# Cross attention of prompt and samples, its output projection and the norms behind it as one program on Trainium2

## The reference

```python
def cross_attention(h, mk, mv, w_xq_l, w_xo_l):
    q = (h @ w_xq_l).reshape(B, L, X_HEADS, X_HEAD_DIM)          # 4 heads of 256
    s = jnp.einsum('bqhd,bmhd->bhqm', q, mk) * (X_HEAD_DIM ** -0.5)
    p = jax.nn.softmax(s, axis=-1)                               # over 256 memory tokens
    o = jnp.einsum('bhqm,bmhd->bqhd', p, mv)
    return o.reshape(B, L, D_MODEL) @ w_xo_l

xp = xp + rms_norm(cross_attention(rms_norm(xp, g_pre_x[l]), mk, mv, w_xq[l], w_xo[l]), g_post_x[l])
xs = xs + rms_norm(cross_attention(rms_norm(xs, g_pre_x[l]), cache_mem_k[l], cache_mem_v[l], w_xq[l], w_xo[l]), g_post_x[l])
fp, bufp = conv_ffn(rms_norm(xp, g_pre_ffn[l]), ...)
```

## Time and profile before

| what | value |
|---|---|
| median of 3 runs | 4068.7 us |
| profiled execution, its span | 4069.45 us, 4067.6 us |
| TensorE busy | 3535.1 us (87%) |
| VectorE busy | 2340.0 us (58%) |
| ScalarE busy | 1144.2 us (28%) |
| GpSimd busy | 610.6 us (15%) |
| mean granted TensorE clock | 0.914 |
| DMA moved | 239.69 MB, mean 59 GB/s |

### The profile page before, as it was taken

One profiled execution on the slowest core, in us unless ns is written; L12 is line 12 of the kernel. 1 busy time (PEld: TensorE's weight loads), 2 busy tenths in 40 slices (PEclk: granted clock), 3 DMA queues, 4 the chain that ended last, 5 costly groups with the idle time before them and its releaser, 6 DMA issues. The chain is left out here.

```text
span 4067.6 us, 52580 instructions
## 1 busy us (share of the span) xinstructions
PE 3535.1 (87%) x21828; PEld 3392.4 (83%) x21828; DVE 2340.0 (58%) x3459; ACT 1144.2 (28%) x1607; POOL 610.6 (15%) x254
## 2 busy tenths in 40 slices
PE   6999669968969999999679996698789699999995
PEld 6999459868959999999579994687689599999994
DVE  5776653630046777776777766444300566776776
ACT  4432443330032222222144415342301322222221
POOL 1111121100101222222011111201001021221210
PEclk8999789985789999999889997899858899999997
DMA  3112122204101111111021121322041011111111
GB/s 149 38 45 67 60 93 91 71 32 145 44 23 39 45 47 47 47 47 48 6 101 43 44 74 49 130 63 78 12 166 32 14 47 47 47 42 47 42 51 44
DMA packets 56596, 239.69 MB, mean 59 GB/s; under 512 B 7584, under 2 KB 9888, under 8 KB 50080
## 3 DMA queue, kind: packets, MB, share of 16 engines
q1 hardware_dynamic: 55776, 236.03, 17.9%
q10 hardware_dynamic: 576, 0.24, 0.0%
HBM read 207.91 MB, written 23.04 MB: 57 GB/s over the span
## 5 line engine op out<-in xcount | busy, mean ns | idle before, releaser
L225 PE MATMUL ps<-hh,w_hi 128*128 128x344 f32 (+2 forms) x4320 | 1415.9, 328 | 188.2 <-DVE hl L1206 70.5
L226 PE MATMUL ps<-hl,w_hi 128*128 128x344 f32 (+2 forms) x4320 | 1395.2, 323 | 0.0
L227 PE MATMUL ps<-hh,w_lo 128*128 128x344 f32 (+2 forms) x4320 | 1394.8, 323 | 0.0
L210 POOL TENSOR_TENSOR w_lo<-w_raw,w_hi 128x1024 fp32r<-128x1024 f32 x250 | 610.4, 2442 | 3364.1 <-ACT w_hi L202 3364.1
L225 PEld LDWEIGHTS ps<-hh,w_hi 128*128 128x128 f32 x4320 | 826.1, 191 | 215.4 <-issue 173.4
L226 PEld LDWEIGHTS ps<-hl,w_hi 128*128 128x128 f32 x4320 | 825.8, 191 | 1.2
L227 PEld LDWEIGHTS ps<-hh,w_lo 128*128 128x128 f32 x4320 | 825.0, 191 | 0.0
L2148 DVE TENSOR_TENSOR Y<-Y,ps 128x344 f32<-128x344 f32 x1008 | 478.9, 513 | 170.7 <-PE ps L227 170.4
L202 ACT ACTIVATE w_hi<-w_raw 128x1024 fp32r<-128x1024 f32 x276 | 289.6, 1051 | 507.1 <-PE ps L227 415.9
L225 PE MATMUL ps<-f_ghi,w_hi 128*128 128x344 f32 x1056 | 339.6, 322 | 20.0 <-DVE f_glo L2133 20.0
L227 PE MATMUL ps<-f_ghi,w_lo 128*128 128x344 f32 x1056 | 340.6, 323 | 0.0
(11 more groups left out here) (298 smaller groups left out, 4065.3 us busy)
## 6 DMA issues: line engine op xcount, KB each, us to landing
w_raw<-in_w_stream SPq DMA_DIRECT2D x276, 512.0 KB, 3.6
xs_cache<-in_cache_mem_k SPq DMA_DIRECT2D x16, 1024.0 KB, 5.0
xs_cache<-in_cache_mem_v SPq DMA_DIRECT2D x16, 1024.0 KB, 4.8
out_y_cols<-xT SPq DMA_DIRECT2D x3, 4128.0 KB, 13.8
xT<-out_y_cols SPq DMA_DIRECT2D x2, 4128.0 KB, 15.2
xT<-in_x_cols SPq DMA_DIRECT2D x1, 4128.0 KB, 14.7
hg<-Y SPq DMA_DIRECT2D x32, 129.0 KB, 2.4
xT<-in_state_hgrn SPq DMA_DIRECT2D x8, 512.0 KB, 3.7
```

The costliest lines, as they stand in the source:

```text
L210: nc.gpsimd.tensor_tensor(w_lo[:, SLOT[m], :], w_raw[:, m % RR, :], w_hi[:, SLOT[m], :].bitcast(F32), ALU.subtract).then_inc(lo_done["pool ...
L225: nc.tensor.matmul(out, whi, mhi, start=start, stop=False)
L226: nc.tensor.matmul(out, whi, mlo, start=False, stop=False)
L227: return nc.tensor.matmul(out, wlo, mhi, start=False, stop=stop)
```

## The change

The stages `stage_cross`, `stage_cross_samples`, `stage_project("xo")` and `stage_norm("n2")` are replaced by one stage, `stage_cross_output`. `attention_blocks` and `stage_project` are gone. In detail:

- The loads of `mkT` and `mv` move into `stage_output_query`, between slab loads on SP's queue.
- The prompt's attention goes over 16 units (a group of 128 tokens and two of the heads). Scores stay in PSUM: maximum and exponentials read them there, and the copy with scale is gone. The products with the values are made for two groups at once (256 columns).
- The `xo` projection is made in the three column runs of `C3`, so 24 units. From attention unit 8 on, one unit of the first run stands behind each attention unit. The slabs are visited up, down and up again (`xo_slab`); with three held, 18 slabs are loaded per layer where 8 were.
- The samples' queries are laid into a zeroed tile `qm` of 32 columns per sample, of which only 4 (one per head) are not zero. A sample's scores are 8 float32 matmuls with this tile as stationary operand and 256 key tokens as moving columns, all samples accumulating into one 32 x 256 PSUM tile; its values are 4 matmuls of 512 columns with a tile `pm` made the same way from the probabilities. The result is turned back by 8 transposes (`sample_out`).
- The caches of the samples come through two buffers, which are the memory of `mkT` and `mv` (`cache(t)` is the one or the other), once these are no longer read. This work stands between units of the second column run.
- The norms' sums are made as in `stage_output_query`: squares out of PSUM, sums over blocks on VectorE, and one matmul with ones per run (`mean`, six in all).

The diff, cut, with the indentation of the new stage reduced:

```diff
+def xo_slab(n):
+    c, i = divmod(n, KT)
+    return KT - 1 - i if c == 1 else i
...
-    v += [(("xo", k), S_XO + k) for k in range(KT)]
+    v += [(("xo", xo_slab(n), n // KT), S_XO + xo_slab(n)) for n in range(3 * KT)]
...
+        load_slabs(sp, l, LOAD_OF[VISIT["xq", 0, 0]] + 1)
+        sp.dma_start(mkT[:], io["mem_k"][l]).then_inc(mem_in, 16)
+        load_slabs(sp, l, LOAD_OF[VISIT["xq", 3, 0]] + 1)
+        sp.dma_start(mv[:], io["mem_v"][l]).then_inc(mem_in, 16)
         load_slabs(sp, l, fits_after(end) + RR)
+        sp.wait_ge(mem_in, 32)
...
+def stage_cross_output(l, mkT, mv):
...
+        def caches(t):
+            if t >= 2:
+                sp.wait_ge(s["s_done"], t - 1)
+            elif t == 1:
+                sp.wait_ge(s["pv"], 32)
+            else:
+                sp.wait_ge(s["scores"], n)
...
+        load_slabs(sp, l, first)
+        caches(0)
+        caches(1)
+        load_slabs(sp, l, first + 2)
+        for t in range(2, 2 * NS):
+            caches(t)
+            if t in (4, 6, 8):
+                load_slabs(sp, l, first + t // 2 + 1)
+            if t in (10, 12):
+                load_slabs(sp, l, second + t // 2 - 4)
+        load_slabs(sp, l, fits_after(end) + RR)
...
+        def scores(u):
+            g, hp = divmod(u, 2)
+            if u >= 2:
+                pe.wait_ge(s["exp"], u - 1)
...
+        def turn(u):
+            pe.wait_ge(s["probs"], u + 1)
...
+        def values(p):
+            pe.wait_ge(s["copied"], 4 * p + 4)
             for k in range(KT):
+                i = KT * p + k
+                if i >= 2:
+                    pe.wait_ge(s["out_lo"], i - 1)
                 for a in range(2):
+                    last = nc.tensor.matmul(ps[:, 4 + i % 2, 0:256], mv[:, a, P * k:P * k + P], PT[:, a, k // 2, :],
+                                            start=(a == 0), stop=(a == 1))
+                last.then_inc(s["pv"], 1)
...
+        def unit(c, i):
...
+            pe.wait_ge(s["out_lo"], (16, 24, 32)[c])
+            if c == 2:
+                pe.wait_ge(s["s_lo"], 1)
+            if u >= 2:
+                pe.wait_ge(s["out"], u - 1)
...
+            for k in range(KT):
+                last = nc.tensor.matmul(ps[0:32, 0, 0:NMEM], qm[:, k, 32 * t:32 * t + 32], keys[:, k, :],
+                                        start=(t == 0 and k == 0), stop=(t == NS - 1 and k == KT - 1))
...
+            for a in range(2):
+                for h in range(2):
+                    last = nc.tensor.matmul(ps[0:32, 4 + h, :], pm[:, a, 32 * b:32 * b + 32],
+                                            v[:, a, 512 * h:512 * h + 512],
+                                            start=(b == 0 and a == 0), stop=(b == NS - 1 and a == 1))
...
+        scores(0)
+        scores(1)
+        for u in range(n):
+            turn(u)
+            if u + 2 < n:
+                scores(u + 2)
+            if u and u % 4 == 0:
+                values(u // 4 - 1)
+            if u >= 8:
+                unit(0, u - 8)
+        values(3)
+        for i in range(4):
+            unit(1, i)
+            if i == 0:
+                mean(0)
+            sample_scores(2 * i)
+            sample_scores(2 * i + 1)
+        unit(1, 4)
+        sample_turn()
+        unit(1, 5)
+        for t in (8, 9, 10):
+            sample_values(t)
+        unit(1, 6)
+        for t in (11, 12, 13, 14, 15):
+            sample_values(t)
+        mean(1)
+        unit(1, 7)
+        sample_out()
+        unit(2, 0)
+        mean(2)
+        for i in range(1, KT):
+            unit(2, i)
+        mean(3)
+        mean(4)
+        mean(5)
...
+        def exps(u):
+            act.wait_ge(s["negmax"], u + 1)
+            if u >= 3:
+                act.wait_ge(s["turned"], u - 2)
+            q = small[:, u % 4]
+            for j in range(2):
+                last = nc.scalar.activation(S[u % 3][:, j, :], ps[:, u % 2, NMEM * j:NMEM * j + NMEM], ACT.Exp,
+                                            bias=q[:, 1, j:j + 1], scale=scale, accum_out=q[:, 2, j:j + 1])
+            last.then_inc(s["exp"], 1)
+        def copy(u):
...
+            if u >= 4:
+                act.wait_ge(s["pv"], KT * (u // 4))
...
+        def high_of_values(p):
+            for k in range(KT):
+                i = KT * p + k
+                act.wait_ge(s["pv"], i + 1)
+                nc.scalar.activation(hh[:, k, 256 * p:256 * p + 256], ps[:, 4 + i % 2, 0:256], ACT.Copy)\
+                    .then_inc(s["out_hi"], 1)
...
+        def evacuate(c, i):
+            u = KT * c + i
+            wait_unit(act, c, i)
+            src = ps[:, 6 + u % 2, 0:C3[c][1]]
+            square(("post", c, i), src)
+            nc.scalar.activation(Y[:, xo_slab(u), cols(c)], src, ACT.Copy).then_inc(s["out"], 1)
+            split_hi(act, fits_after(VISIT["xo", xo_slab(u), c] + 1))
...
+        evacuate(2, 0)
+        root(2)
+        for i in range(1, 6):
+            evacuate(2, i)
+        high(1)
+        evacuate(2, 6)
+        evacuate(2, 7)
+        root(3)
+        squares(1, range(KT))
+        root(4)
+        high(2)
+        squares(2, range(KT))
+        root(5)
...
+        def top(u):
+            dve.wait_ge(s["scores"], u + 1)
+            q = small[:, u % 4]
+            dve_c(nc.vector.tensor_reduce(q[:, 0, :], ps[:, u % 2, :].rearrange("p (j k) -> p j k", j=2), AX.X,
+                                          ALU.max))
+            nc.vector.tensor_scalar(q[:, 1, :], q[:, 0, :], -scale, None, ALU.mult).then_inc(s["negmax"], 1)
+        def share(u):
+            dve.wait_ge(s["exp"], u + 1)
+            q = small[:, u % 4]
+            dve_c(nc.vector.reciprocal(q[:, 3, :], q[:, 2, :]))
+            nc.vector.tensor_tensor(S[u % 3], S[u % 3], over_cols(q[:, 3, :], NMEM), ALU.mult)\
+                .then_inc(s["probs"], 1)
+        def low_of_values(p):
+            for k in range(KT):
+                i = KT * p + k
+                dve.wait_ge(s["out_hi"], i + 1)
+                at = (slice(None), k, slice(256 * p, 256 * p + 256))
+                nc.vector.tensor_tensor(hl[at], ps[:, 4 + i % 2, 0:256], hh[at].bitcast(F32), ALU.subtract)\
+                    .then_inc(s["out_lo"], 1)
...
+        top(0)
+        top(1)
+        share(0)
+        for u in range(n):
+            if u + 2 < n:
+                top(u + 2)
+            if u + 1 < n:
+                share(u + 1)
+            if u and u % 4 == 0:
+                low_of_values(u // 4 - 1)
...
+        normalise(2)
+        add(("post", 2, 1))
+        residual(1, range(0, 4))
+        add(("post", 2, 2))
+        add(("post", 2, 3))
+        residual(1, range(4, KT))
+        add(("post", 2, 4))
+        add(("post", 2, 5))
+        low(1, range(0, 4))
+        add(("post", 2, 6))
+        add(("post", 2, 7))
+        normalise(3)
+        residual(2, range(KT))
+        adds(1, range(1, KT))
+        low(1, range(4, KT))
+        scale_of(4)
+        low(2, range(KT))
+        adds(2, range(1, KT))
+        scale_of(5)
...
-        stage_output_query(l)
-        clear_semaphores(False)
         mkT = cross.enter_context(nc.sbuf_tensor("mkT", [P, KT, NMEM], F32))
         mv = cross.enter_context(nc.sbuf_tensor("mv", [P, 2, D], F32))
-        stage_cross(l, mkT, mv)
-    stage_cross_samples(l)
-    stage_project("xo", l, VISIT["xo", 0], N_XO, False, False)
+        stage_output_query(l, mkT, mv)
+        clear_semaphores(False)
+        stage_cross_output(l, mkT, mv)
     clear_semaphores(False)
-    stage_norm("n2", l, G_POST_X, G_PRE_FFN, VISIT["a", 0])
```

More of the change, by code:

```diff
@@ L1979, in _ @@
[L1979 to L1982 removed]
+                        def scores(u):
[3 more added lines that the diff above has]
+                            for j in range(2):
+                                for d in range(2):
+                                    k = 4 * hp + 2 * j + d
+                                    last = nc.tensor.matmul(ps[:, u % 2, NMEM * j:NMEM * j + NMEM], Y[:, k, P * g:P * g + P],
+                                                            mkT[:, k, :], start=(d == 0), stop=(d == 1))
+                            last.then_inc(s["scores"], 1)
@@ new lines, in mean, with sample_scores @@
+                        def mean(i):
+                            kind, c = MEANS[i]
+                            pe.wait_ge(s["acc_used"], sums_before((kind, c, KT - 1)) + 1)
+                            if i:
+                                pe.wait_ge(s["root"], i)
+                            nc.tensor.matmul(ps[:, 3, 0:C3[c][1]], ones[:], acc[:, c, 0:C3[c][1]], start=True, stop=True)\
+                                .then_inc(s["mean"], 1)
+                        def sample_scores(t):
+                            if t == 0:
+                                pe.wait_ge(s["q_ready"], 1)
+                            pe.wait_ge(kv_in[t % 2], 16 * (t // 2 + 1))
+                            keys = cache(t).rearrange("p (k t) -> p k t", k=KT)
+                            for k in range(KT):
```

(23 more changed lines are left out.)

474 lines of the change are left out of this document (200 added, 274 removed).

## The result

The changed kernel took 3867.05 us (median of 4 runs, 3861.3 to 3873.28), the kernel before 4063.02 us beside it: ratio 0.9516, 95% interval 0.9488 to 0.9544, so 196 us less. Three later groups of runs gave it 3865.3, 3863.0 and 3866.46 us (ratios 0.9511, 0.9504 and 0.9505). The forecast was 3882 us, 187 us less.

The account below looks back on a forecast made before the run. TensorE, busy 313 of 390 us per layer, was slowed by low-clock one-column matmuls and waits. Stage terms summed to 294.4 us, 93.6 less per layer after 2 for loads, 187.2 for both: 3882 us, range 3840 to 3960.

Parts of the forecast that it names:

- units 0 to 7: Prompt attention alone on TensorE, rounds of 4.4 us: 54 us per layer, bounds 47 and 75 (clock at 1.2 GHz).
- units 8 to 15, last values: Attention units each followed by a projection unit covering VectorE; TensorE is the bound: 74.7 us per layer.
- second run with the samples: Second column run, samples' work between projection units: units 33.7, samples 57.5, plus late caches and split waits; 99.3 us per layer.
- third run: Last column run: eight projection units of 2.90 us and a mean, seventh and eighth unit 1.4 us late; 25.3 us.
- tail and clearing: After the last unit: ScalarE's slab splits, then VectorE's norm chain, 34.6 us; clearing semaphores and starting the MLP, 6.5 us.
- query projection's stage: Two 1 MB transfers placed between its slab loads delay slabs: 2 us per layer, bounds 0 and 5.
- my two bounds for sparse tiles: Samples' matmuls with 32-column stationary tiles: 57.5 us per layer at 2.4 GHz, or twice that; the lower was taken.
- (a): Rival: sparse tiles in the samples' work run at 1.2 GHz, costing 75 us per layer: 4032 us; 12 in 100.
- (b): Rival: cache buffers and slabs on one queue leave transfers half open, 37 us per layer: 3956 us; 10 in 100.
- (c): Rival: shorter head and tail, caches in time, 19 us per layer less: 3844 us; 10 in 100.
- (d): Rival: whole fused stage stays at 1.2 GHz, slower than before, up to 4316 us; 3 in 100.
- My division of the gain: Of 95.6 us gained per layer, some 55 samples' stage, 25 to 30 norm's, the rest start and overlap.

Follow-up runs that it names:

- the last experiment: Sums over blocks of the last two norms made by TensorE: in the changed kernel alone 3856.24 us, with low parts also moved to VectorE 3839.04 us.
- the experiment: Changed kernel with low parts of eight slabs per layer made by VectorE instead of GpSimd: 3856.57 us, and 3860.2 us when repeated.

## Why the prediction was right

The mechanism was right in its parts. 187 us were forecast and 196 measured, and that the two lie so close is in part luck: errors of 6.6 and 3.5 us per layer, to either side, are in the sum. Per layer, from the first layer's windows above:

| term | forecast | measured |
|---|---|---|
| units 0 to 7 | 54 (47 to 75) | 47.4 |
| units 8 to 15, last values | 74.7 | 73.0 |
| second run with the samples | 99.3 | 99.2 |
| third run | 25.3 | 26.7 |
| tail and clearing | 34.6 + 6.5 | 44.6 |
| sum | 294.4 | 290.9 |
| query projection's stage | + 2 (0 to 5) | 0 |

- **Units 0 to 7** were the largest error. A round is 4.16 us and not 4.4, the start up to the first turning 7.9 and not 9.2, and the clock did not fall, so the 3 us that I had added for a falling clock were not due; at full clock I had 50.7. The rounds from 826.30 on ran at 1.00 (below): waits of 1.78 us in each, with 2.4 us of work, did not take the clock down. The Trainium skill (TensorE: Matmul & The Clock Gate, HAM oscillation) tells of bursts that are shorter than the waits between them; here the wait is the shorter of the two, so it does not speak for the 75 us of my upper bound. Its Part 4 says that transposes don't count as work for the clock; no run here can show it, since each round has matmuls of 1.89 us beside its 0.66 us of transposes.

```profile
826.30:868.89 42.59, 27.84 (x135) 21.17 (x133) 17.86 (x44) 17.43 (x55) 0.00 (x0) 1.00 0.00 1
```

- **Units 8 to 15** are TensorE's work to within 2.3 us (70.75 of 73.02), as forecast; a round is 8.2 us in the mean (forecast 8.3).
- **The samples** held to 0.1 us, with their parts: 3.62 us a sample (I had 3.62 for the keys and 3.56 for the values), three late caches of 1.41 to 1.42 us where I had three of 1.3, and 0.96 us before unit (2, 0). The lower of my two bounds for sparse tiles was the right one, and its reason too: the kind of matmul decides, and not that TensorE is recorded as busy. Nearer rows than those I named were in the trace of the kernel before: float32 matmuls of 512 columns, 0.43 us from one entry to the next (so 0.86 a matmul, against my 0.89), and in the window attention tiles of 64 stationary columns with 256 moving ones at a clock of 1.00:

```profile
156.81 1.88 PE L1089 MATMUL ps<-hg_work,ones 128*128 128x512 f32 x4
459.47 0.65 PE L693 MATMUL ps<-xT,rs 128*64 128x256 f32 x4
```

- **The third run** had two waits of 1.05 and 1.06 us for GpSimd's low parts; I had put one of 1.4 there.
- **The tail** was 3.5 us too low, and that is two errors which partly cancel. VectorE's last reciprocal ends at 1109.28 (below), 41.5 us after the last unit, where I had 34.6; clearing and start then take 3.1 us and not 6.5. ScalarE's idle 5.94 us was the wrong row for them; what made it longer was not followed. Of the 6.9 us, 2.0 are a slip in my addition: the terms that I listed give 28.1, not 26.1. Some 3 are the start. I had ScalarE's slab splits set it, ending 8.5 us after the last unit; in fact the first mean waits 10.33 us for VectorE, whose low part and sums GpSimd's splits had made late. With the low parts on VectorE this wait is 6.96 us and the tail 3.3 us shorter. The rest, 1.8 us, is the chain itself, a little slower than its scaled rows.
- **The query projection** lost nothing to the two loads. I had taken 2 us between bounds of 0 and 5, because ScalarE waits for slabs there; the stretch with the loads in it is as long as without them (211.99 and 211.98 us).

VectorE in the tail of the changed kernel, the chain after the first mean:

```profile
1084.19 3.33 DVE L2088 SCALAR_TENSOR_TENSOR xT<-Y,gT,xT 128x264 f32<-128x264 f32 x8
1087.55 4.53 DVE L2070 TENSOR_TENSOR x_acc<-x_acc,x_sq 128x384 f32<-128x384 f32 x7
...
1097.73 4.20 DVE L2098 SCALAR_TENSOR_TENSOR hl<-xT,gT,hh 128x264 fp32r<-128x264 f32 x8 [0.58 <-ACT hh L1982]
1101.96 3.66 DVE L2070 TENSOR_TENSOR x_acc<-x_acc,x_sq 128x264 f32<-128x264 f32 x7
1107.48 1.80 DVE L2105 RECIPROCAL rs<-x_rt 128x264 f32<-128x264 f32 x1 [1.85 <-ACT x_rt L1976]
```

The sums (4.53 and 3.66) are what the last experiment moved to TensorE.

So one layer gained 390.0 - 290.9 = 99.1 us, and twice that is 198. The medians differ by 196 and the two profiled executions by 208, because the one of the kernel before was 6.4 us above its median and that of the changed kernel 5.8 below; so 198 and 196 agree better than the traces bear out. Of the 10 us between 198 and 208, 2.2 are the earlier start of the first stage, and some 7 lie between the two layers' stages (1213.74 to 2843.40 before, 1112.42 to 2735.23 after the earlier trace rows), in code that the change doesn't touch. Scatter it is hardly: the four profiled executions of the changed kernel lie within 1.0 us of each other there, and the kernel with sparse tiles alone takes as long as the kernel before up to its load of `mkT` (1629.6 and 1629.7 us). I found no cause for the 7.

**The rivals.** (a), sparse tiles at the lower clock, is refuted by both kernels that isolate it (sparse tiles alone, all samples in one piece): the tiles bring the clock to 1.00 by themselves. (b), open transfers, holds only for three of 16 caches; it grows when the units between are taken away, but transfers are only 4.7 of the 21 us that this costs in the first layer. (c) was right for units 0 to 7 by its number only, for it put 47 us to rounds of 4.4 us at full clock, which by my own sum make 50.7, and the rounds were shorter; for the tail and for the caches it was wrong. (d) is nowhere: the clock's mean over the whole stage is 0.92, and the only part below 0.95 is the tail (0.55), in which TensorE is busy 4 us. (Its 217 us of TensorE's work are 218 by the terms listed.)

My division of the gain holds roughly: 55 us per layer for the samples (sparse tiles alone gave 55.5), 25 to 30 for the norm (put apart again it cost 25.4 in its own stretch and 23.5 in the time). The parts are no fixed shares, though: taken out of the changed kernel, the same tiles are worth 35 us per layer, because one-column matmuls between dense units still run at the upper clock for part of their time.

## What to carry to other kernels

Ask of a stage that is full of small matmuls at which clock they run before counting them: here 16 of one column and 8 of 256 cost the same at the upper clock, and the wide ones win only because they hold it. Filling a stage's gaps with another stage's work is worth what the gaps hold of waits for other engines, and the softmax between two products can count for more than the transfers. When a fused stage ends in a chain on one engine, look for parts of it that an idle engine can make, and for a neighbour that slows it down.

## What the runs showed of the hardware

VectorE and GpSimd held each other up, which I had not reckoned with. VectorE in the changed kernel, with the same instruction first without and then with a neighbour, and the sums and residual of the third run; then GpSimd at those times:

```profile
828.32 0.17 DVE L2046 TENSOR_SCALAR x_small<-x_small 128x2 f32<-128x2 f32 x1
...
887.88 2.35 DVE L2046 TENSOR_SCALAR x_small<-x_small 128x2 f32<-128x2 f32 x1
...
1052.36 2.50 DVE L2070 TENSOR_TENSOR x_acc<-x_acc,x_sq 128x264 f32<-128x264 f32 x1
1054.78 4.34 DVE L2088 SCALAR_TENSOR_TENSOR xT<-Y,gT,xT 128x384 f32<-128x384 f32 x4
```
```profile
887.82 2.40 POOL L216 TENSOR_TENSOR w_lo<-w_raw,w_hi 128x1024 fp32r<-128x1024 f32 x1 [70.14 <-ACT w_hi L208]
...
1049.50 7.61 POOL L216 TENSOR_TENSOR w_lo<-w_raw,w_hi 128x1024 fp32r<-128x1024 f32 x2 [1.15 <-ACT w_hi L208]
```

An instruction on 2 elements a partition takes 2.35 us instead of 0.17, because a split of 2.40 us had started 0.06 us before it. An addition takes 2.50 instead of 0.43, and four residuals 4.34 instead of 2.20 (with GpSimd idle, in the experiment). GpSimd loses too: two splits last 7.61 us where two alone last 4.8. So it is no sharing in proportion; one waits for the other's whole instruction. The Trainium skill (SBUF — State Buffer, Who interferes with whom) says just this of VectorE instructions with two SBUF inputs or in a mode that uses both ports, and the rows agree; had I applied it, GpSimd's splits in the third run would have been a term of the tail. By the same rows the low parts on VectorE cost less than they look: 1.22 us there, against 2.4 us in which both engines were tied up.
